# Attention of layer 0: exponentials and copies of ScalarE take turns, transposes wait head by head

## The reference, cut to what matters

```
main:    q (16 heads of 64), k, v (4 heads) of 512 positions; key blocks of 128
         s = q k^T / 8 over the blocks before, at and after its own (masked |kpos-qpos| <= 128)
             and over the 2 context blocks
context: s = q k^T / 8 over the 2 context blocks
p = softmax([s, sink]);  o = p v;  y = o @ w_o
```

## Time and profile before

| | us |
|---|---|
| median of 3 runs | 3875.13 (3872.19 to 3875.18) |
| the profiled execution, its own time | 3889.61 |
| its span | 3887.8 |
| TensorE busy in the span | 3510.5 (90%) |
| VectorE busy | 2062.1 (53%) |
| ScalarE busy | 1508.4 (39%) |
| GpSimd busy | 221.6 (6%) |

### The profile page before, as it was taken

How to read it: one execution, slowest core, us unless ns; L and a number is a source line. 1 busy time by engine, 2 the same in 40 slices (tenths; PEclk the granted TensorE clock), 3 DMA queues, 4 the chain that set the end, 5 groups by cost and what they waited for, 6 DMA issues and landing times.

```text
span 3887.8 us, 59821 instructions
## 1 busy us (share of the span) xinstructions
PE 3510.5 (90%) x24660; PEld 2758.4 (71%) x24660; DVE 2062.1 (53%) x3400; ACT 1508.4 (39%) x2750; POOL 221.6 (6%) x431
## 2 busy tenths in 40 slices
PE   6877799999989986787989999789999989799999
PEld 4744378888876766777668887666888666568886
DVE  4365444334456755775554455855444645454446
ACT  5466632222234643333433332534333424443334
POOL 0011000000000003333300000000000000000000
PEclk8989999999999996999999999879999999899999
DMA  4111113332114577776322232102222221022221
GB/s 191 39 65 45 65 55 132 140 120 98 65 44 149 161 170 181 169 185 151 116 82 98 87 109 75 58 27 77 98 90 97 74 74 55 32 73 97 98 98 54
DMA packets 294413, 378.22 MB, mean 97 GB/s; under 512 B 240448, under 2 KB 243392, under 8 KB 259584
## 3 DMA queue, kind: packets, MB, share of 16 engines
q1 hardware_dynamic: 280912, 328.78, 26.3%
q10 hardware_dynamic: 13232, 45.61, 3.5%
HBM read 330.30 MB, written 44.06 MB: 96 GB/s over the span
## 4 chain that ended last, share of the span: by engine, by line
PE 79%; DVE 9%; ACT 6%; issue 3%; DMA 2%; POOL 0%; SPq 0%; ACTq 0%; DVEq 0%; POOLq 0%
PE ps L257 18%; PE ps L258 18%; PE ps L259 18%; PE ps L776 2%; PE ps L1319 1%; PE ps L1321 1%; PE ps L1320 1%; DVE wlo L249 1%; ACT s L807 1%; PE ps L766 1%; PE ps L339 1%; PE ps L2164 1%; PE ps L2146 1%; PE ps L2840 1%; PE ps L2174 1%
## 5 line engine op out<-in xcount | busy, mean ns | idle before, releaser
L242 ACT ACTIVATE whi<-panel 128x512 fp32r<-128x512 f32 (+1 forms) x517 | 435.2, 842 | 587.7 <-PE ps L259 573.8
L249 DVE TENSOR_TENSOR wlo<-panel,whi 128x512 fp32r<-128x512 f32 (+1 forms) x517 | 495.7, 960 | 238.9 <-ACT whi L242 230.3
L257 PE MATMUL ps<-dh,whi 128*128 128x512 f32 (+1 forms) x1280 | 474.2, 370 | 0.0
L258 PE MATMUL ps<-dh,wlo 128*128 128x512 f32 (+1 forms) x1280 | 471.3, 368 | 0.0
L259 PE MATMUL ps<-dl,whi 128*128 128x512 f32 (+1 forms) x1280 | 471.0, 368 | 0.0
L257 PE MATMUL ps<-xh,whi 128*128 128x512 f32 x1088 | 443.8, 408 | 25.1 <-DVE xl L2881 18.8
L258 PE MATMUL ps<-xh,wlo 128*128 128x512 f32 x1088 | 430.5, 396 | 0.0
L259 PE MATMUL ps<-xl,whi 128*128 128x512 f32 x1088 | 429.5, 395 | 0.0
L257 PE MATMUL ps<-hh,whi 128*128 128x512 f32 (+1 forms) x960 | 351.4, 366 | 27.9 <-DVE hl L460 27.7
L258 PE MATMUL ps<-hh,wlo 128*128 128x512 f32 (+1 forms) x960 | 338.9, 353 | 0.0
L259 PE MATMUL ps<-hl,whi 128*128 128x512 f32 (+1 forms) x960 | 338.4, 352 | 0.0
(11 more groups left out here) (540 smaller groups left out, 5867.1 us busy)
## 6 DMA issues: line engine op xcount, KB each, us to landing
panel<-in_w SPq DMA_DIRECT2D x246, 1024.0 KB, 4.8
late<-s_fe ACTq DMA_DIRECT2D x16, 1024.0 KB, 5.6
late<-s_fe ACTq DMA_DIRECT2D x48, 256.0 KB, 4.0
s_fe<-x SPq DMA_DIRECT2D x24, 256.0 KB, 3.2
late<-s_fe ACTq DMA_DIRECT2D x8, 768.0 KB, 6.1
s_fe<-xx SPq DMA_DIRECT2D x16, 256.0 KB, 2.7
s_fe<-ctx SPq DMA_DIRECT2D x24, 128.0 KB, 2.7
s_ia<-panel SPq DMA_DIRECT2D x24, 128.0 KB, 4.5
```

The costliest lines, as they stand in the source:

```text
L242: e.activation(unit(u)[0][:, 0:kc, :], w, ACT.Copy).then_inc(*w_hi.up(u))
L249: e.tensor_tensor(lo[:, 0:kc, :], w, hi[:, 0:kc, :].bitcast(F32), SUB).then_inc(*w_lo.up(u))
L257: e.matmul(out, hi[:, k, :], xh, start=k == 0, stop=False)
L258: e.matmul(out, lo[:, k, :], xh, start=False, stop=False)
```

## The change

ScalarE's function `soft` is cut into `exps(n, i)`, one head at a time, and `out` into `turned(n, j)`, one block at a time; all steps now go exponential i of unit n-1, copy i of unit n-2, for i from 0 to 3, and then the fifth copy if there is one. The small exponential belongs to the fourth exponential. The ada row's copy stands behind all of it. On TensorE the one wait for the fourth head's probabilities becomes a wait for each head ahead of its transpose in the first block.

```diff
@@ TensorE, out(n)
-            e.wait_ge(*at_dv.at("prob", n, 3))
             nb = len(blocks)
             for j in range(nb + 2):
                 if j < nb:
...
                     for i in range(4):
+                        if j == 0:
+                            e.wait_ge(*at_dv.at("prob", n, i))
                         x = e.transpose(B[4 + t % 2][:, i * P:i * P + P], S4[n % 3][:, i, j * P:j * P + P], ID)
@@ ScalarE
-        def soft(n):
+        def exps(n, i):
             nb, s, sm = len(AUNITS[n][2]), S4[n % 3], NSM[:, n % 3, :, :]
-            e.wait_ge(*at_dv.at("neg", n))
-            for i in range(4):
-                e.activation(s[:, i, 0:nb * P], s[:, i, 0:nb * P], ACT.Exp, bias=sm[:, i, 1:2],
-                             accum_out=sm[:, i, 2:3]).then_inc(*at_ac.up("exp", n, i))
-            e.wait_ge(*at_dv.at("es", n))
-            e.activation(sm[:, :, 3], sm[:, :, 3], ACT.Exp).then_inc(*at_ac.up("es", n))
-
-        def out(n):
-            for j in range(len(AUNITS[n][2])):
+            if i == 0:
+                e.wait_ge(*at_dv.at("neg", n))
+            e.activation(s[:, i, 0:nb * P], s[:, i, 0:nb * P], ACT.Exp, bias=sm[:, i, 1:2],
+                         accum_out=sm[:, i, 2:3]).then_inc(*at_ac.up("exp", n, i))
+            if i == 3:
+                e.wait_ge(*at_dv.at("es", n))
+                e.activation(sm[:, :, 3], sm[:, :, 3], ACT.Exp).then_inc(*at_ac.up("es", n))
+
+        def turned(n, j):
+            if j < len(AUNITS[n][2]):
                 t = TBASE[n] + j
@@ ScalarE, the loop
-            if n not in ASTEP and n > 1:
-                out(n - 2)
-            if 0 < n <= NAU:
-                soft(n - 1)
+            for i in range(4):
+                if 0 < n <= NAU:
+                    exps(n - 1, i)
+                if n > 1:
+                    turned(n - 2, i)
+            if n > 1:
+                turned(n - 2, 4)
...
             if n in ASTEP:
-                if n > 1:
-                    out(n - 2)
                 ada_row(e, ASTEP[n])
```

## The result

The changed kernel took 3840.49 us (median of 4 runs, 3837.97 to 3844.68), the kernel before 3875.15 in the same comparison: ratio 0.991, 95% interval 0.9893 to 0.9927, so 28 to 41 us faster. Run again later beside other kernels it had 0.9898 (0.9884 to 0.9912). The forecast was 3833 with 3815 to 3853.

What follows compares the result with a forecast made beforehand. The prediction took engines waiting on each other in the attention as the bound, TensorE mostly for ScalarE's copies. Terms 24.0 + 4.4 + 2.3 + 8.2 + 4.5 - 1.0 gave 42 us, hence 3833 us, range 3815 to 3853.

Steps and rivals of the forecast that it cites:

- B steps: Attention loop steps that follow A steps; forecast to take 7.5 us each, four-block ones 6.9 to 7.7.
- C steps: Attention loop steps that follow B steps; forecast to take 12 to 12.5 us each, four-block ones 9 to 10.
- A steps: Attention loop steps handling a main unit after a context unit; forecast to take 11.3 us between ends of products.
- (1): A steps: exponentials between copies let VectorE scale earlier, so the next scores wait 1.1 us less, eight times.
- (2): B steps: second copy comes earlier; with the A gain, 3.6 us shorter for five blocks, 3.2 for four, 24.0 in all.
- (3): C steps: net 0.5 us gained in six where GpSimd's subtraction meets the scalings, 1.4 in step 23; 4.4 us.
- (4): End of the attention: waits in the last two passes go, 2.0 us; step 2 gives 0.3 us.
- (5): TensorE's clock: slow product blocks vanish in B steps and at the end, 8.2 us; half of 9.0 in C, 4.5.
- (6): TensorE's 72 extra head-by-head waits cost 1 us, with bounds of nothing and 3.6 us.
- Rival (a): Attention: the order helps, the clock does not, slow blocks reappear elsewhere; 30 us gained, 3845; chance 0.20.
- Rival (b): B's gain turns into waiting in C because ScalarE is in debt; 14 us gained, 3861; chance 0.08.
- Rival (d): A and C: copies at the exponentials' pace split TensorE's work, keeping its clock low; slower by 46, 3921; chance 0.05.

Runs made afterwards that it cites:

- B alone: New ScalarE order in B steps only, with the head-by-head waits, other steps as in the kernel before; 3857.4 us, 0.9958 of the kernel before.
- C alone: New ScalarE order in C steps only, with the head-by-head waits, other steps as in the kernel before; 3853.58 us, 0.9945 of the kernel before.
- stands filled: Kernel before, with the ada product repeated in B and C steps (three times for five blocks, twice for four); 3858.5 us, 0.9956.
- queries behind the copies: Changed kernel, with ScalarE's queries copy in C steps put behind all copies of line 820; 3827.84 us, 0.9877 of the kernel before.
- the two runs with moved queries: Changed kernel, ScalarE's queries in C steps moved behind the scores' copies (3829.69 us, 0.9872) or behind all copies (3827.84 us, 0.9877).

## Why the prediction was right, step by step

The forecast was 42 us; the two profiled attentions differ by 40.7, the medians by 35 (28 to 41) and, in the later comparison, 38. So the sum fits the profiled execution that it was read from, and stands 4 to 7 us above the medians: its clock terms were counted in an execution of the kernel before that took 14.5 us more than the median. The kernel with the head waits alone, as fast as the one before, had 259.16 us of attention in an execution at its median, 38.5 more than the change.

From end to end of the products, as the forecast counts (the table counts from copy to copy), the seven B steps became 29.7 us shorter (forecast 24.0 and 6.8 of clock), the seven C steps 8.1 (4.4 and 4.5), the end 3.4 (2.0 and 1.4), and the A steps 0.4 longer in all: TensorE waits 0.31 us for 0.25 behind their first copy, the exponential ahead of it that was taken as nothing. Its terms, in its order:

(1) A, 1.1 us: right. The wait of the earlier trace rows fell from 1.70 to 0.61 us, and the A step itself kept its length (11.45 us for 11.51).

(2) B, 3.6 us shorter from end to end for five blocks, 7.5 us left: right. Products end at 324.26 and 331.84, 7.58 us. The pause from a copy to the next exponential that I had chosen as 0.55 us was 0.48 (328.83 to 329.31 in the same timeline); small exponential and debt came as worked out (0.9 us late for 1.1).

(3) C, a net 0.5 us because GpSimd's subtraction falls into the scalings: right in place and size. One scaling of four takes 1.5 to 1.6 us ahead of each of the six C steps named, and nowhere else from step 2 on. Scalings 2.95 us for 1.94, and with the queries moved each C step lost 1.0 us and nothing else. What the working missed is that the ada product also waits for the ada addition, queued on VectorE behind the scalings (0.24 us). Without the collision that chain, and not the first copy, ends last, which is why moving the queries out of ScalarE's way gave nothing more and my expectation for that run was 0.5 us a step too high. Also, the cost is larger than these 6 us in the total: without the collision the clock fell in one or no C step instead of three, and the attention got 8.8 to 10.5 us shorter.

(4) The end, 2.0 us and 1.4 of clock: 13.44 to 10.03 us, 3.4. In size both are right: three kernels with the old order there and the full clock took 12.09 us. But those three (B alone, C alone, stands filled) also say that the clock's 1.4 us is not owed to the waits alone that the new order removes, for the waits were still there (1.62 and 0.77 us, or 0.92 and 1.09) and the clock stayed up.

(5) The clock, 8.2 us in B and at the end and half of 9.0 in C: right. No B step and not the end was slow in any kernel with the new order in A and B, and three of six C steps were. The half was the middle between two bounds and not worked out, so that it came out as three of six is in part luck; without the head waits it was two. That the term exists apart from the order is shown by the filled stands, where the old order alone won 16.4 us in the attention, of the 17.2 that I had read as paid (14.2 against the execution with the head waits alone).

(6) The waits, 1 us: nothing was measured, 0.9997 and equal A steps.

Rival (a), no help from the clock, gave 3845, and the median of 3840.49 lies nearer to it than to 3833; but its mechanism, slow blocks that come back elsewhere, is not in the traces and falls with (5); (c), hidden behind, with the total. Rival (b), B's gain turned into waiting in C, lost as a forecast but holds a truth that my sum did not show: new C steps after an old B take 10.42 us and after a new B 11.7. B's new order beside the other two shortened B by 14.8 us (71.50 to 56.70) and lengthened C by 13.1 (66.52 to 79.63), and brought 1.7 us in all. Of those 13.1 the collision and its slow clock are 8.8 to 10.4, by the two runs that remove it; the rest fits the chain of scalings, ada addition and ada product, which a shorter B lets reach into C (seen in the run with the queries behind the copies). Rival (d), the clock kept down by short pieces of work, is refuted for A and B. What the rule that the prediction cites from the Trainium skill ("TensorE: Matmul & The Clock Gate", "Part 4: PE-mode transpose") would need did not show: with the collision gone the same sparse transposes stand ahead of C, and no C step was slow in one run and one in another. What the two runs took away was about 1 us of standing. Whether transposes count less than products for the clock was not tried by itself.

## What to carry to other kernels

When a reordering removes a wait, list what now runs at the same time that did not before: the scaling and GpSimd's subtraction had met at length in one place only the earlier trace rows, and six more such meetings, with the slower clock behind them, kept back 8.8 to 10.5 us, which one moved line returned. Read a stand of TensorE twice: its length, and the slower clock behind it, which in the execution before cost 0.9 to 1.7 us each at a dozen places. Parts of a reordering don't add up: alone, the new order in A, B and C shortened the attention by 12.9, 25.4 and 26.7 us, 65 together for 40.7. Try them apart, because here two of the three kinds of step gave 39.0 of the 40.7 us.

## What the hardware showed that was not expected

Three ada products in place of one, 2.8 us of TensorE work for 1.07, made the old kernel 17 us faster. A stand alone doesn't decide: of the seven old B steps two stood 2.8 us and ran at the full clock, and the end of the attention ran at either clock behind the same waits. After 2 to 2.5 us, bare (ScalarE's order alone) or with two or three transposes in it (the change, twice), C fell in eight of eighteen cases; with the transposes spread over some 2 us and stands of 0.2 around them it fell once in twelve (the two runs with moved queries). And of four VectorE scalings that meet GpSimd's subtraction only one is longer, by about 1.0 us (1.55 for 0.55 in step 14), and it ends behind the other engine's operation; that one took 1.26 to 1.51 us in the six meetings, for 1.27.
